# A 16-pair recurrence whose round is rearranged on every engine, and one attention head whose scores are formed in full float32

## The reference, cut to what matters

```python
def dsa_sparse_attention(q, k, v, q_idx, k_idx, w_idx):
    ...
        s = jnp.einsum('bqhd,bqnhd->bqhn', qb, kg).astype(jnp.float32) * att_scale
        s = jnp.where(sel_ok[:, :, None, :], s, -jnp.inf)
        p = jax.nn.softmax(s, axis=-1)
...
def wkv7_scan(r, w, k, v, kk, a):
    def step(state, inp):
        r_t, w_t, k_t, v_t, kk_t, a_t = inp
        sa = jnp.einsum('bhvk,bhk->bhv', state, -kk_t)
        state = (state * w_t[:, :, None, :]
                 + sa[..., None] * (kk_t * a_t)[:, :, None, :]
                 + v_t[..., None] * k_t[:, :, None, :])
        return state, jnp.einsum('bhvk,bhk->bhv', state, r_t)
...
    decay = jnp.exp(-jnp.exp(w_log))
    a = jax.nn.sigmoid((a0 + (xa @ a1) @ a2).astype(f32))
    kk = kk / jnp.maximum(jnp.sqrt(jnp.sum(kk * kk, axis=-1, keepdims=True)), L2_EPS)
    k = k * (1.0 + (a - 1.0) * k_a)
    o = wkv7_scan(r, decay..., k..., v..., kk..., a...)
    o = ((o - mean) * lax.rsqrt(var + GN_EPS)).reshape(B_, S, D) * gn_w + gn_b
    bonus = jnp.sum(r * k * r_k, axis=-1, keepdims=True) * v
    o = (o + bonus.reshape(B_, S, D)) * jax.nn.silu(g)
    return o.astype(x.dtype) @ w_o
```

## Time and profile before

| | |
|---|---|
| median of the runs | 3493.98 us |
| the profiled execution | 3500.6 us, span 3498.8 us, clock 0.984 |
| PE busy | 3364.9 us (96%) |
| DVE, ACT, POOL busy | 1818.4, 1408.5, 415.1 us |
| pair 0's chunk products begin (line 1699) | 2881.23 us |
| pair 13's, 14's and 15's | 3212.04, 3240.84, 3267.56 us |
| the last projection begins (line 294) | 3285.57 us |

### The profile page before, as it was taken

The page is one execution under the profiler, slowest core; times in us unless marked ns, Lnnn a source line. Parts: engine busy times, 40 slices in busy tenths (PEclk is TensorE's granted clock), DMA queues, the critical chain, the costliest instruction groups (busy, mean ns, idle before and its releaser), DMA issues.

```text
span 3498.8 us, 51676 instructions
## 1 busy us (share of the span) xinstructions
PE 3364.9 (96%) x21012; PEld 2673.5 (76%) x21012; DVE 1818.4 (52%) x2380; ACT 1408.5 (40%) x1616; POOL 415.1 (12%) x718
## 2 busy tenths in 40 slices
PE   7899999999999999999999999999999988999897
PEld 1566888888887788888887867888888866777785
DVE  5745666666667333444423457242424247777445
ACT  1323344344434223444423236141414167777423
POOL 0000222322122000000000000000000023444000
PEclk9999999999999999999999999999999999999898
DMA  9522232333233442222222313333333333332321
GB/s 351 184 73 80 98 102 90 108 102 102 99 104 102 139 145 85 84 84 84 84 90 90 132 62 134 124 122 121 120 120 120 134 93 83 71 88 61 126 97 72
DMA packets 178956, 381.46 MB, mean 109 GB/s; under 512 B 111728, under 2 KB 117104, under 8 KB 145008
## 3 DMA queue, kind: packets, MB, share of 16 engines
q1 hardware_dynamic: 164352, 326.73, 28.3%
q0 software_dynamic: 14448, 52.50, 4.4%
HBM read 342.49 MB, written 35.13 MB: 108 GB/s over the span
## 4 chain that ended last, share of the span: by engine, by line
PE 85%; DVE 4%; DMA 3%; POOLq 3%; SPq 2%; issue 1%; ACT 1%; DVEq 1%; POOL 0%; ACTq 0%
PE PJ L294 18%; PE PJ L296 18%; PE PJ L295 18%; PE AB L294 6%; PE AB L296 6%; PE AB L295 6%; POOLq L1582 1%; POOLq L1579 1%; PE AB L233 1%; DMA WK<-ada 1%; PE AB L681 1%; DMA X<-blocks_scratch 1%; PE AB L1677 1%; PE AB L1686 1%; PE AB L447 1%
## 5 line engine op out<-in xcount | busy, mean ns | idle before, releaser
L294 PE MATMUL PJ<-XH,WH 128*128 128x512 f32 x2848 | 1127.5, 396 | 17.2 <-DVE XL L421 10.3
L296 PE MATMUL PJ<-XH,WL 128*128 128x512 f32 x2848 | 1111.7, 390 | 0.0
L295 PE MATMUL PJ<-XL,WH 128*128 128x512 f32 x2848 | 1110.9, 390 | 0.0
L325 DVE TENSOR_TENSOR WL<-RAW,WH 128x2048 fp32r<-128x2048 f32 (+2 forms) x239 | 543.1, 2273 | 695.3 <-ACT WH L320 691.4
L320 ACT ACTIVATE WH<-RAW 128x2048 fp32r<-128x2048 f32 (+2 forms) x240 | 453.6, 1890 | 914.9 <-PE PJ L296 655.0
L294 PEld LDWEIGHTS PJ<-XH,WH 128*128 128x128 f32 x2848 | 536.2, 188 | 142.4 <-issue 29.7
L296 PEld LDWEIGHTS PJ<-XH,WL 128*128 128x128 f32 x2848 | 535.9, 188 | 113.3
L295 PEld LDWEIGHTS PJ<-XL,WH 128*128 128x128 f32 x2848 | 536.4, 188 | 109.6 <-issue 1.9
L294 PE MATMUL AB<-XH,WH 128*128 128x512 f32 (+1 forms) x960 | 380.9, 397 | 10.0 <-DVE XL L421 7.7
L295 PE MATMUL AB<-XL,WH 128*128 128x512 f32 (+1 forms) x960 | 375.0, 391 | 0.0
L296 PE MATMUL AB<-XH,WL 128*128 128x512 f32 (+1 forms) x960 | 375.0, 391 | 0.0
(11 more groups left out here) (448 smaller groups left out, 3880.5 us busy)
## 6 DMA issues: line engine op xcount, KB each, us to landing
RAW<-w SPq DMA_DIRECT2D x232, 1024.0 KB, 4.9
WK<-ada SPq DMA_DIRECT2D x32, 1024.0 KB, 6.5
GATE<-gate POOLq DMA_DIRECT2D x64, 256.0 KB, 3.1
rkvg_scratch<-WK POOLq DMA_DIRECT2D x16, 1024.0 KB, 4.7
x_scratch<-X POOLq DMA_DIRECT2D x8, 1024.0 KB, 5.9
X<-rkvg_scratch SPq DMA_DIRECT2D x32, 256.0 KB, 3.7
RAW<-rkvg_scratch SPq DMA_DIRECT2D x32, 256.0 KB, 3.5
X<-xT SPq DMA_DIRECT2D x4, 1024.0 KB, 15.8
```

Source lines behind the costliest of these rows:

```text
L294: nc.tensor.matmul(bank[0:width, n, :], hi, xh, start=first, stop=False)
L295: nc.tensor.matmul(bank[0:width, n, :], hi, xl, start=False, stop=False)
L296: m = nc.tensor.matmul(bank[0:width, n, :], lo, xh, start=False, stop=last)
L325: nc.vector.tensor_tensor(WL[k % 2][:, :, 0:w], narrow(RAW[k % 2], w), WH[k % 2][:, :, 0:w].bitcast(F32), ALU.subtract).then_inc(wl_ready, 1)
```

## The change

It has two parts. In the attention, for head 7 alone, ACT's copy and DVE's subtraction are dropped and PE forms the scores from the float32 q and k themselves, one product for each row block in place of three. In the recurrence, every engine's list for a row is rewritten, and the counts that the waits use with it. All seven hops of a pair now stand in the row of its chunk products. SP issues the blocks of pair v + 2 at the start of its round and the solved blocks of the same pair at its end. Cut to its core:

```diff
             elif k == 2:
+                if is_last(h):
+                    pe.wait_ge(s("at_roped"), 2 * h + 1)
+                    for b in range(TB):
+                        m = nc.tensor.matmul(AB[:, b, 0:ROW_W[b]], wk(4)[:, b * P:(b + 1) * P], wk(5)[:, 0:ROW_W[b]],
+                                             start=True, stop=True)
+                    m.then_inc(s("at_scores"), 1)
+                    return
...
-                wait(act, s("at_roped"), 2 * h + 1)
-                nc.scalar.activation(AT_HI, wk(4, 2), ACT.Copy).then_inc(s("at_sd"), 1)
+                if not is_last(h):
+                    ...
-                wait(dve, s("at_sd"), 2 * h + 2)
-                nc.vector.tensor_tensor(AT_LO, wk(4, 2), AT_HI.bitcast(F32), ALU.subtract).then_inc(s("at_roped"), 1)
+                if not is_last(h):
+                    ...
...
         def wv_sp(sp, t):
-            at(t + 1, lambda q: sp_solved_out(sp, q), 1)
             at(t + 2, lambda q: sp_blocks_out(sp, q), 2)
-            at(t + 3, lambda q: sp_load_lora(sp, q), 3)
+            at(t + 3, lambda q: sp_load(sp, q), 3)
             at(t + 1, lambda q: sp_solved_back(sp, q), 1)
             at(t + 2, lambda q: sp_blocks_in(sp, q), 2)
+            at(t + 3, lambda q: sp_load_lora(sp, q), 3)
             at(t + 2, lambda q: sp_levels(sp, q), 2)
-            at(t + 4, lambda q: sp_load(sp, q), 4)
+            at(t + 2, lambda q: sp_solved_out(sp, q), 2)
...
         def pe_token_d(pe, q):
-            pe.wait_ge(wv("factors"), 4 * q + 1)
+            pe.wait_ge(wv("factors"), 4 * q + (2 if q else 1))
...
         def pe_fg(pe, t):
+            pe.wait_ge(wv("pq_sb"), t + 1)
             pe.wait_ge(wv("masked"), 3 * min(t + 2, PAIRS))
...
         def pe_oa(pe, t):
-            pe.wait_ge(wv("pq_sb"), t + 1)
+            pe.wait_ge(wv("masked"), 3 * min(t + 2, PAIRS - 1) + 1)
...
         def act_sig_rate(act, q):
+            A(ws(T_A), bank(3), ACT.Sigmoid, bias=col("a0", q))
+
+        def act_sig_decay(act, q):
             act.wait_ge(wv("lora"), q + 1)
-            A(ws(T_A), bank(3), ACT.Sigmoid, bias=col("a0", q))
-
-        def act_sig_decay(act, q):
             wait(act, wv("bonus"), q)
             A(ws(T_LOGW), bank(2), ACT.Sigmoid, bias=col("w0", q)).then_inc(wv("sig"), 1)
```

More of the change, by code:

```diff
@@ L453, in build, with is_last @@
         AT_HI, AT_LO = WK_R[:, 10 * SEQ:12 * SEQ], WK_R[:, 4 * SEQ:6 * SEQ]
+        def is_last(h):
+            return isinstance(h, int) and h == HEADS - 1
         def att_pe(pe, h, k):
@@ L498, in att_act @@
             elif k == 2:
-                wait(act, s("at_roped"), 2 * h + 1)
-                nc.scalar.activation(AT_HI, wk(4, 2), ACT.Copy).then_inc(s("at_sd"), 1)
+                if not is_last(h):
+                    wait(act, s("at_roped"), 2 * h + 1)
+                    nc.scalar.activation(AT_HI, wk(4, 2), ACT.Copy).then_inc(s("at_sd"), 1)
                 wait(act, s("at_masked"), h + 1)
@@ L1476, in exp_done @@
         def exp_done(q, i):
-            return 4 * q + ((1, 2, 3, 4) if q == 0 else (1, 2, 3, 4) if q == 1 else (3, 1, 2, 4))[i]
+            return 4 * q + ((1, 2, 3, 4) if q == 0 else (1, 2, 4, 3))[i]
         def sig_done(q):
@@ L1484, in key_logged @@
         def key_logged(q):
-            return (3, 6)[q] if q < 2 else 4 * q
+            return (3, 6)[q] if q < 2 else 4 * q + 2
         def key_ready(q):
@@ L1492, in gate_ready @@
         def gate_ready(q):
-            return 2 if q == 0 else min(4 * q + 6, 4 * PAIRS)
+            return 2 if q == 0 else 4 * q + 4
         def sp_load(sp, q):
@@ L1592, in pe_lora @@
             wait(pe, wv("masked"), 3 * q - 2)
+            wait(pe, wv("oa_sb"), q - 2)
             nc.tensor.matmul(bank(2), LW2(q)[:, 0:P], TW[0:LORA, :], start=True, stop=True)
@@ L1647, in pe_nt @@
             pe.wait_ge(wv("factors"), 4 * q + 2)
-            wait(pe, wv("oa_sb"), q - 1)
             pe_pairs(pe, q, T_D, 2, wv("nt"))
@@ L1690, in pe_pq @@
         def pe_pq(pe, t, f):
-            if f == 1:
+            if f == 0:
                 pe.wait_ge(wv("inverse"), 3 * t + 3)
-            else:
                 pe.wait_ge(wv("bv"), min(t + 2, PAIRS))
@@ L1805, in wv_pe @@
             at(t + 1, lambda p: pe_hop(pe, p, 2))
-            at(t + 3, lambda p: pe_token_d(pe, p), 1)
             at(t + 1, lambda p: pe_hop(pe, p, 3))
-            at(t + 4, lambda p: pe_lora(pe, p), 2)
-            at(t + 1, lambda p: pe_hop(pe, p, 4))
+            at(t + 3, lambda p: pe_token_k(pe, p), 1)
+            at(t + 1, lambda p: pe_hop(pe, p, 4))
+            at(t + 4, lambda p: pe_ss(pe, p), 2)
+            at(t + 1, lambda p: pe_hop(pe, p, 5))
+            at(t + 2, lambda p: pe_level_w(pe, p, 0))
+            at(t + 1, lambda p: pe_hop(pe, p, 6))
+            at(t + 3, lambda p: pe_token_e(pe, p), 1)
+            at(t + 1, lambda p: pe_hop(pe, p, 7))
+            at(t + 2, lambda p: pe_level_y(pe, p, 0))
+            at(t + 4, lambda p: pe_lora(pe, p), 2)
+            at(t + 3, lambda p: pe_bonus(pe, p), 1)
+            at(t + 2, lambda p: pe_level_w(pe, p, 1))
+            at(t + 3, lambda p: pe_bt(pe, p))
+            at(t + 2, lambda p: pe_level_y(pe, p, 1))
+            at(t + 4, lambda p: pe_token_v(pe, p), 1)
         A = nc.scalar.activation
@@ L1858, in act_gate @@
         def act_gate(act, q):
+            wait(act, wv("gs"), q)
             A(ws(T_SG), ws(T_IN(q) + T_G), ACT.Sigmoid).then_inc(wv("keys"), 1)
@@ L2033, in dve_level_x, with dve_reff @@
             nc.vector.transpose(ws(T_X), YT(v)).then_inc(wv("inverse"), 1)
+        def dve_reff(dve, t):
+            dve.wait_ge(wv("products"), 2 * t + 1)
+            V(by_parity(ws(T_REFF)), by_parity(ws(RR_OF(t))), quarter(6, CH), ALU.subtract)
         def dve_factors(dve, t):
@@ L2037, in dve_factors @@
                 dve.wait_ge(wv("y_zero"), 2)
-            dve.wait_ge(wv("products"), 2 * t + 1)
-            V(by_parity(ws(T_REFF)), by_parity(ws(RR_OF(t))), quarter(6, CH), ALU.subtract)
             for h in range(2):
@@ L2543, in _ @@
                 wv_act(act, t)
+            act_r1(act, PAIRS - 1)
+            act_level(act, PAIRS - 1, 0)
+            act_oa(act, PAIRS - 2)
             act_level(act, PAIRS - 1, 1)
```

114 lines of the change are left out of this document (48 added, 66 removed).

## The result

The changed kernel takes 3531.99 us (median of 4 runs, 3526.80 to 3534.19), where the kernel before takes 3496.73 us on the same chip (4 runs, 3491.92 to 3501.32). The ratio is 1.0099, with a 95% interval of 1.0079 to 1.0118: 35 us slower, where 6.5 us faster was forecast and 3504 us was the end of the range. The profiled execution took 3532.84 us (span 3531.0 us, clock 0.983), so the spans of the two profiles differ by 32.2 us.

What follows compares the result with a forecast made beforehand. PE, busy 96% of the span, was taken as the bound, so only its stalls could be won. Head -4.4, rows +7.2, ends -9.3, start 0 gave -6.5: 3487.5 us from 3493.98, range 3472 to 3504.

Steps and rivals of the forecast that it cites:

- The head: Attention head: PE's 3.62 us stall and the slow clock behind it go, float32 product costs more; -4.4 us.
- The rows: Middle recurrence rows, pair 0 to 13: 26.0 us each for 25.45, +7.2 us over 13 rows; chance 0.47.
- the sum of the stalls: PE's stalls (a), (b) and (c) in a recurrence row: 3.35 us on 22.5 of work, a row of 25.87.
- the upper bound of the row: Recurrence row of 27.2 us if a pair's load, sharing DMA engines with the blocks, lands 1.2 us late each time.
- The clock: Rival: stalls of 1.2 and 1.5 us slow PE's clock in every row, 4 us each; 3540 us, chance 0.07.
- (a): Before the second y product: PE stalls 1.15 us for ACT's level copy, behind a table load waiting for the bonus.
- (b): Between `fg` and hop 1: PE stalls 1.5 us for DVE, 4.5 us of DVE's work against 3.0 of PE's.
- (c): The hops: PE stalls 0.38 us between hops 2 and 3, 0.32 before hop 4; hop to next hop 0.81.
- ACT as the bound: Rival: ACT, with 23.6 us of work a row, is late at each release; row 27.2, 3503 us, chance 0.12.
- the extreme: ACT's rival at its worst: each table switch costs twice its row, 32.6 us a row, 3573 us; 2 in 100.
- The queue's loop: Loop through SP and POOL: falls from 25.8 to 24.7 us, under PE's row; POOL's wait shorter than 11 us.
- The ends: Rows of pairs 13 and 14 fall to 23.0 and 23.2 us, pair 15's stays 18.0; together -9.3 us.

Runs made afterwards that it cites:

- run 2: Changed kernel with the load of a pair issued almost a row earlier and DVE's gate product at its row's start: 3494.16 us, ratio 1.0005.
- run 4: Changed kernel with the load a row earlier, DVE's gate product at the row's start, and the rate's sigmoid before the decay's: 3484.31 us, ratio 0.9977.
- run 1: Kernel before with the attention head's edit alone, its recurrence unchanged: 3484.25 us, ratio 0.9982.
- run 5: Kernel before with SP's new round and start alone, old lists of PE, DVE and ACT: 3619.25 us, ratio 1.0355.

## Why the prediction was wrong

*The head* was right: -4.7 for -4.4, the stall and the slow clock behind it gone. (After reached the head 0.5 us later than before, so the stretch around it shrank by 5.2.) The one figure without a row, the float32 product, was 1.76 us for the 2.4 estimated.

*The rows* are the step that failed, +46.6 for +7.2, and in a known place. The prediction wrote that "in the queue's loop the load of a pair (four DMAs) takes the place of the small weights, at about the same time to issue". It counted the load as issue time for SP and never walked when its data are wanted. In its own terms that takes one subtraction: issue some 7 us into the row, the square of the key some 12 us into it, 5.0 us between; and before, 6.3 us had been between. Nor is the time to issue the same: the load took 2.0 to 3.9 us in the middle rows of after, where the small weights took 0.65 (3145.38) to 1.73 (3120.23) in before, and the solved blocks stand behind it. So the sum of the stalls, 3.35 us, had no term for the load. The runs showed 2.5 us a row in that place (28.71 against 26.19 in run 2): 1.5 of PE's wait for the key and 0.9 of the slow clock. The subtraction alone would have found 0.6 us of lost lead in the mean row; of a landing that is itself later, by 1 us and more, only the two late rows of before gave a hint. The prediction did name the mechanism, as the upper bound of the row: "if the load of a pair, which now shares the DMA engines with the blocks, lands 1.2 us late each time". In the row shown it lands 2.56 us late for ACT and 2.08 us late for PE.

*The clock* was held apart as a rival of its own, with a chance of 0.07. Its point of decision was put between stalls of 0.65 and 2.53 us, and its price at 4 us a row; the price in after was 0.9 us a row. After every wait for the key of 2.0 us or more, PE ran at half rate within the next few groups. Behind PE's waits of 1.2 us in run 2 (15 of them) the clock stayed at 1.00. In between, the length of the wait does not decide. In after, seven of the twelve middle rows are hit, among them one behind a wait of 0.91 us, while a wait of 1.41 us left the full rate (1.97 us against 1.12 for the same two matmuls):

```profile
3150.99 1.12 PE L1612 MATMUL AB<-X,MAT 128*128 128x512 f32 x2 [1.41 <-ACT X L1838]
...
3237.36 1.97 PE L1612 MATMUL AB<-X,MAT 128*128 128x512 f32 x2 [0.91 <-ACT X L1838]
```

What else decides is not shown here. The Trainium skill (TensorE: Matmul & The Clock Gate, HAM oscillation) tells of a kernel whose repeated wait keeps lowering the clock; in after the trace agrees, though only some rows are hit, and the mean is 0.97. The late load and the slow clock are not independent cases: once the load is 2 us late the second follows. Had the upper bound been worked out as 2 us of wait and 1 us of clock, the row would have stood at 29.0 and the sum at 3493.98 - 13.7 + 13 x 3.55 = 3526 us, 6 us under the time.

*Stalls (a) and (b)* were right. (a) was 1.2 us a row for 1.15 walked, from the table load that carries the wait, and removing it gave 0.65 us a row once the load was in time (run 4 against run 2). (b) was 1.2 us in two places for 1.5 in one. (c) shows in no row of waits, but in a row of run 2 hops 2 and 3 start 0.81 us apart, as walked:

```profile
3015.51 0.43 PE L1756 MATMUL AB<-WS 128*128 128x64 f32 x2
...
3016.32 0.43 PE L1756 MATMUL AB<-WS 128*128 128x64 f32 x2
```

With the load in time the walked row of 25.87, taken as 26.0, is measured at 26.19.

*ACT as the bound* did not come: a row has 23.9 us of ACT's work in 28.7 us. Nor did the extreme, a switch at twice its row: behind a table load of 1.28 us the ACTIVATE starts at once (3047.23 and 3048.53 above). On this the Trainium skill (ScalarE: Activation LUTs, What ACT_TABLE_LOAD costs) is right with the load's 1283 ns, and its drain of about 1380 ns shows in no row here: in the recurrence of after, each of the 102 loads is followed by its ACTIVATE within 0.02 us.

*The queue's loop* did not get to decide. POOL stood 12.67 us before the solve shown, not under 11: the row is long for other reasons, so the solves come less often.

*The ends* came near, -7.5 for -9.3, but by luck. Pair 13's row is 23.07 us, as walked (23.0), and PE's stall of the earlier trace rows is gone; pair 14's is 22.40 for 23.2, pair 15's 20.59 for 18.0. But the gain is measured against one execution with a slow clock (0.76 over these three rows). With the old order run 1 took 64.9 us from pair 13's chunk products to the last projection (3201.08 to 3266.00, clock 0.92), and run 5, with the old lists too, 64.9 (3341.48 to 3406.41), where the profile of before took 73.5 and that of after 66.1. In run 1 PE's stall for the inverse of pair 14 was still there, 2.15 us. So none of the 7.5 us is shown to come from the new order. A stretch with a fallen clock should not be carried from a single profile.

*What stays open* is how much of the late landing each neighbour makes. That the landings of the solved blocks and blocks in go from 3.4 and 3.2 us to 4.6 and 4.5 with the load among them, and back to 3.3 and 3.2 in run 2, is shown. So is that the DMA engines are full or nearly so in that stretch. But in run 5, with the same round of SP and the old lists, the load was complete 5.7 to 7.7 us after its first issue (6.3 in the mean of the twelve rows), for 7.6 in after. Why the new lists add to it was not found. The load's own medians, DMA by DMA, rise less (from 3.5 to 3.9 and 3.6 us); it is the last of the four that ACT waits for.

## What to carry to other kernels

For every DMA that a change moves in a queue, write down four moments in the new order: when its destination is free, when it is issued, when it lands amid its new neighbours, and when it is first read. A lead that just suffices looks like almost no wait in the profile (here two rows of twelve showed it). With 0.6 us less of it, and transfers of other kinds issued right around the load, ACT waited 2 us in the mean row, and PE's clock fell in seven rows of twelve. And ask of each small instruction that moves whose buffer it frees: the one that nobody waits for (here the gate product) may hold the next load.
